# A two-layer decoder trunk: the even mixer's recurrent part is put in another order

## What is computed

```python
for i in range(DEPTH):                       # layer 0 is even, layer 1 odd; 512 tokens, width 1024
    x = x + 0.5 * swiglu(rms_norm(x, ffn1_norm[i]), ffn1_w_gu[i], ffn1_w_down[i])
    hn = rms_norm(x, mix_norm[i])
    if i % 2 == 0:
        proj = hn @ even_w_in[j]
        ya = sliding_window_attention(qa, ka, va, swa_sinks[j])          # 8 heads, 2 kv heads
        yb = rwkv7_time_mix(hb, ...)                                     # 8 heads of 64
        mixed = jnp.concatenate([ya, yb], axis=-1) @ even_w_out[j]
    else:
        mixed = forgetting_attention(qc, kc, vc, log_f) @ fox_w_out[j]
    x = x + mixed
    x = x + 0.5 * swiglu(rms_norm(x, ffn2_norm[i]), ffn2_w_gu[i], ffn2_w_down[i])
    x = x + jax.nn.sigmoid(rms_norm(x, ple_norm[i]) @ ple_w_gate[i]) * (p[i] @ ple_w_proj[i])
return rms_norm(x, final_norm)

def step(state, inp):                        # inside rwkv7_time_mix, over the tokens
    r_t, w_t, k_t, v_t, kk_t, a_t = inp
    s_kk = jnp.einsum('bhij,bhj->bhi', state, kk_t)
    state = (state * w_t[:, :, None, :] - s_kk[..., None] * (kk_t * a_t)[:, :, None, :]
             + v_t[..., None] * k_t[:, :, None, :])
    return state, jnp.einsum('bhij,bhj->bhi', state, r_t)
```

## Time and profile before

| | |
|---|---|
| median of three runs | 2234.67 us (2231.94 to 2236.96) |
| the profiled execution's own time | 2235.76 us |
| its span | 2234.1 us |
| TensorE busy | 2147.3 us, 96% of the span |
| VectorE, ScalarE, GpSimd busy | 1126.0, 746.0, 347.8 us |
| share of TensorE in the chain that ended last | 92% |
| mean granted TensorE clock | 0.981 |

### The profile page before, as it was taken

How to read it: one execution, slowest core, us unless ns; L and a number is a source line. 1 busy time by engine, 2 the same in 40 slices (tenths; PEclk the granted TensorE clock), 3 DMA queues, 4 the chain that set the end, 5 groups by cost and what they waited for, 6 DMA issues and landing times.

```text
span 2234.1 us, 32237 instructions
## 1 busy us (share of the span) xinstructions
PE 2147.3 (96%) x12522; PEld 1746.5 (78%) x12522; DVE 1126.0 (50%) x1337; ACT 746.0 (33%) x968; POOL 347.8 (16%) x352
## 2 busy tenths in 40 slices
PE   7999999996868999999999999999999899999998
PEld 6888888775857888888887888887667688888887
DVE  4443445556685644344565433445666454424464
ACT  4432223343122333122254422223444343312234
POOL 2000004444130300000330000013333320000032
PEclk9999999997979999999999999999999999999999
DMA  5323324320000433332333334324322143243232
GB/s 152 94 80 109 95 84 113 95 57 20 4 2 12 132 94 82 106 107 79 86 111 91 95 92 113 94 71 109 94 75 66 57 132 101 83 118 94 67 94 85
DMA packets 365116, 192.29 MB, mean 86 GB/s; under 512 B 9694, under 2 KB 362064, under 8 KB 365024
## 3 DMA queue, kind: packets, MB, share of 16 engines
q1 hardware_dynamic: 362784, 185.10, 30.0%
q0 software_dynamic: 2224, 5.86, 0.8%
q10 hardware_dynamic: 16, 0.00, 0.0%
HBM read 188.81 MB, written 2.13 MB: 85 GB/s over the span
## 4 chain that ended last, share of the span: by engine, by line
PE 92%; DVE 5%; ACT 2%; issue 1%; DMA 0%; POOL 0%; SPq 0%; ACTq 0%; POOLq 0%; DVEq 0%
PE bank L427 24%; PE bank L428 24%; PE bank L429 24%; PE bank L1182 3%; PE bank L1683 2%; PE bank L1685 2%; PE bank L1684 2%; PE bank L795 2%; PE bank L797 2%; PE bank L796 2%; PE bank L1700 1%; PE bank L1719 1%; PE bank L1730 1%; DVE w_lo L417 1%; ACT w_hi L412 1%
## 5 line engine op out<-in xcount | busy, mean ns | idle before, releaser
L427 PE MATMUL bank<-xn_hi,w_hi 128*128 128x512 f32 x1416 | 554.9, 392 | 10.9 <-DVE w_lo L2190 6.0
L428 PE MATMUL bank<-xn_hi,w_lo 128*128 128x512 f32 x1416 | 552.6, 390 | 0.0
L429 PE MATMUL bank<-xn_lo,w_hi 128*128 128x512 f32 x1416 | 552.4, 390 | 0.0
L412 ACT CAST w_hi<-w_raw 128x2048 fp32r<-128x2048 f32 (+3 forms) x211 | 336.3, 1594 | 624.0 <-PE bank L429 560.1
L417 DVE TENSOR_TENSOR w_lo<-w_raw,w_hi 128x2048 fp32r<-128x2048 f32 (+3 forms) x209 | 441.6, 2113 | 151.2 <-ACT w_hi L412 149.8
L427 PEld LDWEIGHTS bank<-xn_hi,w_hi 128*128 128x128 f32 x1416 | 266.9, 188 | 69.5 <-DVE w_lo L2190 6.3
L428 PEld LDWEIGHTS bank<-xn_hi,w_lo 128*128 128x128 f32 x1416 | 266.8, 188 | 56.1 <-issue 1.0
L429 PEld LDWEIGHTS bank<-xn_lo,w_hi 128*128 128x128 f32 x1416 | 266.8, 188 | 55.7
L429 PE MATMUL bank<-h_lo,w_hi 128*128 128x512 f32 x704 | 273.9, 389 | 0.0
L427 PE MATMUL bank<-h_hi,w_hi 128*128 128x512 f32 x704 | 273.9, 389 | 0.0
L428 PE MATMUL bank<-h_hi,w_lo 128*128 128x512 f32 x704 | 273.9, 389 | 0.0
(11 more groups left out here) (345 smaller groups left out, 2624.3 us busy)
## 6 DMA issues: line engine op xcount, KB each, us to landing
w_raw<-in_ffn_w_gu_dram SPq DMA_DIRECT2D x176, 512.0 KB, 5.0
w_raw<-in_ffn_w_down_dram SPq DMA_DIRECT2D x64, 384.0 KB, 3.9
w_raw<-in_ffn_w_down_dram SPq DMA_DIRECT2D x64, 320.0 KB, 3.7
w_raw<-in_even_w_in_dram SPq DMA_DIRECT2D x20, 512.0 KB, 4.5
w_raw<-in_ple_w_gate_dram SPq DMA_DIRECT2D x16, 512.0 KB, 3.8
w_raw<-in_fox_w_in_dram SPq DMA_DIRECT2D x16, 512.0 KB, 5.2
w_raw<-in_even_w_out_dram SPq DMA_DIRECT2D x16, 256.0 KB, 3.2
w_raw<-in_fox_w_in_dram SPq DMA_DIRECT2D x16, 256.0 KB, 4.3
```

The lines of the kernel that those rows point to most:

```text
L412: nc.scalar.copy(w_hi[slot][:, 0:tiles], w_raw[slot][:, 0:tiles]).then_inc(w_hi_ready, 1)
L427: nc.tensor.matmul(dst, w[0], hi[:, k], start=k == 0, stop=False)
L428: nc.tensor.matmul(dst, w[1], hi[:, k], start=False, stop=False)
L429: last = nc.tensor.matmul(dst, w[0], lo[:, k], start=False, stop=k == tiles - 1)
```

## The change

- **Projections in jobs of 8 tiles**: 20 jobs with one bank each, in place of 10 with two; the lora and hb tiles come in the order in which the front of half 0 needs them (`HB_TILES`). `FIRST_WINDOW, APART` become 27, 22.
- **Front of half 0** is put between the projection groups (`rwkv_front_*`, eight pieces on TensorE at groups 118 to 158, with two banks of its own that all eight pieces use in turn).
- **Front of half 1** is put between the inverse levels of half 0, its eight pieces on TensorE one or two to a level; `ab` and `ak` of half 1 stand inside and behind the chain of states of half 0.
- **Tail of half 0** is put between the inverse levels of half 1.
- **Inverse levels**: the level's mask is applied to A before the product, on GpSimd (`a_level`, ten operations of 128x512 in each half), and the product is only copied, by ScalarE (`x_copied`), where VectorE masked it before.
- **Buffers**: pairs of buffers for the two halves; `we` goes into the levels' buffer `m_x`; products that read two interleaved operands are issued as two of 64 columns.
- **Output projection, both mixers**: the weights of jobs 2 and 3 (and 6 and 7) are loaded and split into the upper half of their slot, so they needn't wait until jobs 0 and 1 are done. Job 0's six first rows are issued inside the last chain of states, job 1's ahead of the last `y_turned`.

The core of the diff:

```diff
+        bk = [placed(behind_projections, "bk0", HEADS_BY_DIM), placed(XN, "bk1", HEADS_BY_DIM)]
+        kr = [placed(behind_swa_v, "kr0", HEADS_BY_DIM), placed(XN + 8, "kr1", HEADS_BY_DIM)]
+        kf0 = [placed(behind_swa_k, "kf0_0", HEADS_BY_TOKEN), placed(Y + 28, "kf0_1", HEADS_BY_TOKEN)]
...
+        am0 = [placed(Y + 8, "am0_0", HEADS_BY_TOKEN), placed(behind_swa_v, "am0_1", HEADS_BY_TOKEN)]
+        am2 = [placed(Y + 24, "am2_0", HEADS_BY_TOKEN), placed(behind_swa_v + 4, "am2_1", HEADS_BY_TOKEN)]
+        bonus = [[placed(W + 44 + 2 * q, f"bonus0_{q}", [P, T]) for q in range(2)], [act_out, prod]]
...
+        m_x = placed(XN + 16, "m_x", [P, 2, 2, NC, C])
+        mt_inv = placed(XN + 24, "mt_inv", HEADS_BY_TOKEN)
+        a_lev = placed(XN + 28, "a_lev", HEADS_BY_TOKEN)
+        akm = placed(SCRATCH + 8, "akm", [P, 2, 2, NC, C])
...
+            for n, j, slot, _ in out_jobs(st):
+                e.wait_ge(w_ready, n - 1 if j < 2 else n - 3)
+                if st.startswith("even") and j in (2, 3):
+                    seen(e, ("gn_normed", "y_weighted")[j - 2], 1, 1)
+                loaded = (w_loaded_upper if upper(j) else w_loaded)[slot]
                 for k in (0, DT // 2):
-                    load_tiles(e, n, slot, k, DT // 2, rows[:, k:k + DT // 2, ds(j * P, P)])
+                    first = upper(j) * DT + k
+                    e.dma_start(w_raw[slot][:, first:first + DT // 2],
+                                rows[:, k:k + DT // 2, j * P:(j + 1) * P]).then_inc(loaded, 16)
...
-                return bank[(2, 6)[j]]
+                return bank[(1, 5)[j]]
...
-                product(out_bank_of(st, j, slot)[:], slot, 0, DT, y_hi, y_lo,
+                product(out_bank_of(st, j, slot)[:], slot, upper(j) * DT, DT, y_hi, y_lo,
...
+                if j + 2 < DT:
+                    out_split_hi(act, st, j + 2)
+                    gain_hi(act, norms[st] + 1, j)
...
+                if j + 2 < DT:
+                    out_split_lo(dve, st, j + 2)
...
-        FIRST_WINDOW, APART = 18, 24
+        R_TILE, K_TILE, V_TILE = 0, 1, 2
+        HB_TILES = [(t, 2 * h + q) for h in range(2) for t in (K_TILE, R_TILE, V_TILE) for q in range(2)]
+        LORA_JOB, HB_JOB, EVEN_JOBS = 2 + RP, 4 + RP, 4 + 4 * RP
+        FIRST_WINDOW, APART = 27, 22
...
+            firsts = [SWA_Q, SWA_Q + P] + [a * P for a in range(RP)] + [HB + 3 * RD, HB + 3 * RD + P]
+            firsts += [HB + hb_tile(i) * P for i in range(3 * RP)]
+            for j, col in enumerate(firsts):
+                n = base + j
                 e.wait_ge(w_ready, n - 1)
...
                 for g in range(first, last):
-                    n = base + g // (2 * DT)
-                    slot, k, t = n % 2, g % DT, g % (2 * DT)
-                    if t == 0:
+                    n = base + g // DT
+                    slot, k = n % 2, g % DT
+                    if k == 0:
...
+                    dst = bank[slot][:]
+                    hi, lo = w_hi[slot][:, k], w_lo[slot][:, k]
-                    if t == 2 * DT - 1:
+                    if k == DT - 1:
...
+            front = rwkv_front_tensor(pe, st, 0)
+            between = [(20, value_rows, ())]
             for a in range(RP):
-                begin = 4 * DT + FIRST_WINDOW + APART * a
...
+                begin = FIRST_WINDOW + APART * a
+                between += [(begin, logits, (a, 0)), (begin + 5, logits, (a, 1)),
+                            (begin + 32, transposes, (a, 0)), (begin + 36, transposes, (a, 1)),
+                            (begin + 40, times_values, (a,))]
+            between += [(g, part, ()) for g, part in zip((118, 122, 127, 131, 139, 145, 152, 158), front)]
...
-            for what in "J0 E0 J1 J2 C0 E1 H0 J3 C1 E2 J4 H1 J5 C2 E3 H2 J6 C3 J7 H3".split():
...
+            for what in ("J0 J1 T0 J2 J3 J4 E0 J5 J6 C0 J7 E1 T1 H0 J8 J9 C1 E2 J10 H1 J11 F0 J12 C2 E3 J13 H2 F1 F2 "
+                         "J14 F3 J15 F4 C3 F5 J16 H3 F6 J17 J18 F7 J19").split():
...
-            for what in "J0 L0 J1 D0 L1 J2 D1 V0 J3 M2 L2 J4 M3 D2 V1 L3 J5 M4 D3 V2 J6 M5 J7 M6 V3 M7".split():
...
+            for what in ("J0 J1 J2 L0 J3 J4 D0 J5 L1 J6 J7 T1 D1 V0 J8 L2 J9 M0 J10 M1 V1 D2 L3 J11 M2 J12 M3 V2 "
+                         "J13 M4 D3 M5 F0 J14 F1 F2 J15 F3 M6 F4 V3 J16 F5 M7 F6 F7 F8 J17 M8 F9 J18 M9 F10 "
+                         "J19 M10 M11").split():
...
-            for what in "N0 S2 N1 S3 S4 N2 S5 N3 S6 S7".split():
...
+            for what in "N0 N1 S0 S1 S2 N2 S3 S4 S5 N3 S6 F0 S7 F1 S8 F2 F3 S9 S10 S11".split():
...
+            def ss():
+                for q in range(2):
+                    seen(pe, "kk_squared", h, q)
+                    seen(pe, "v_by_token", h, q)
...
+            def x_copied(h, level):
+                for q in range(2):
+                    level_seen(act, "x", h, level, q)
+                    if level > 1:
+                        level_seen(act, "mxt", h, level - 1, q)
+                    nc.scalar.copy(m_x[:, q, 1], by_chunk(rb(q, 2)[:])).then_inc(R["x_copied"], 1)
...
+            def a_level(h, level):
+                for q in range(2):
+                    if level > 1:
+                        level_seen(pool, "x", h, level - 1, q)
+                    elif h:
+                        level_seen(pool, "x", 0, LEVELS - 1, q)
+                    nc.gpsimd.tensor_tensor(a_lev[:, q], am0[h][:, q], over_chunks(masks[:, MASK_LT + level]),
+                                            ALU.mult).then_inc(R["a_level"], 1)
...
+                ak(0, q)
+            aab(0)
+            f(0)
+            front[0]()
+            xs(0, 1)
+            front[1]()
+            ms(0, 1)
+            front[2]()
+            xs(0, 2)
+            ms(0, 2)
+            front[3]()
+            xs(0, 3)
+            ms(0, 3)
+            front[4]()
+            xs(0, 4)
+            ms(0, 4)
+            front[5]()
+            xs(0, 5)
+            front[6]()
+            ms(0, 5)
+            front[7]()
+            w_and_e(0)
+            gq(0)
+            hs(0)
+            yc(0)
+            z(0, 1)
+            z(0, 2)
+            ab(1, 0)
+            z(0, 3)
+            z(0, 4)
+            ab(1, 1)
+            z(0, 5)
+            z(0, 6)
...
+            f(1)
+            xs(1, 1)
+            yz(0, 0)
+            ms(1, 1)
+            xs(1, 2)
+            yz(0, 1)
+            ms(1, 2)
+            xs(1, 3)
+            g(0)
+            ms(1, 3)
+            xs(1, 4)
+            ms(1, 4)
+            y_turned(0)
+            xs(1, 5)
+            ms(1, 5)
...
+            yc(1)
+            for c in range(1, NC - 1):
+                z(1, c)
+                if c > 1:
+                    out_begin(pe, st, 0, c - 2, c - 1)
+            out_begin(pe, st, 0, NC - 3, OUT_BEGUN["even"])
+            yz(1, 0)
+            yz(1, 1)
+            g(1)
+            out_begin(pe, st, 1, 0, OUT_BEGUN["even"])
+            y_turned(1)
...
+            front = rwkv_front_vector(dve, st, 1)
+            ab_masked(0)
+            ak_masked(0)
+            start_inverse(0)
+            front[0]()
+            level_done(0, 1)
+            front[3]()
+            front[1]()
+            level_done(0, 2)
+            front[4]()
+            front[2]()
+            front[5]()
+            level_done(0, 3)
+            front[6]()
+            front[7]()
+            front[8]()
+            level_done(0, 4)
+            front[9]()
+            front[10]()
+            level_done(0, 5)
+            gq_copied(0)
+            states(0)
+            ab_masked(1)
+            ak_masked(1)
+            start_inverse(1)
...
+            front = rwkv_front_pool(pool, st, 1)
+            start_inverse(0)
+            a_level(0, 1)
+            diag(0)
+            a_level(0, 2)
+            front[0]()
+            a_level(0, 3)
+            a_level(0, 4)
+            front[1]()
+            a_level(0, 5)
+            front[2]()
+            front[3]()
+            start_inverse(1)
+            a_level(1, 1)
+            diag(1)
+            for level in range(2, LEVELS):
```

1257 lines of the change are left out of this document (725 added, 532 removed).

## The result

| | before | after |
|---|---|---|
| median, us | 2234.22 (2231.94 to 2236.96, 4 runs) | 2209.51 (2203.80 to 2211.84, 4 runs) |
| the profiled execution's own time | 2235.76 | 2211.56 |
| its span | 2234.1 | 2209.9 |
| mean granted TensorE clock | 0.981 | 0.989 |

The ratio is 0.9885, 95% interval 0.9861 to 0.9909. The forecast was 2203 us, in a range of 2183 to 2223. Two executions of the later runs, one of the kernel before and one of e11_together, took 2729 and 2752 us at a mean granted clock of 0.745 and 0.731; they are left out of the ratios.

The account below looks back on a forecast made before the run. Prediction: TensorE bounds projections and cores, VectorE and chains between engines bound fronts and tail. Terms -9.4 + 2.5 + 12.1 + 2.6 - 42.5 + 9.3 - 3.1 - 3.3 = -31.8 gave 2203 us, range 2183 to 2223.

Parts of the forecast that it names:

- What stood between the cores: From half 0's chain of states to half 1's first x: 52.5 us falls to about 10, -42.5.
- the third: Rival: the first front doesn't overlap, its shared banks making pieces wait; part 1 takes 184.0, kernel 2224 us; chance 0.08.
- part 1: Projections with the first front: 172.1 us falls to 162.7, -9.4.
- Rivals 2 and 4: VectorE and GpSimd block one another, 2215 us, chance 0.15; GpSimd becomes the bound, 2239 us, chance 0.07.
- The new waits: Waits the new order adds in projections and first front: 19.1 us in all, slow clock included.
- The base: Projections and first front without the new waits: 133.7 us plus 9.9 for the front's matmuls at full clock.
- TensorE stays the bound: Rival: most new waits vanish, part 1 gains 22.5 and levels cost less; kernel 2179 us; chance 0.15.
- the first wait: In the projections, before job 2: TensorE waits 3.2 us for VectorE, 5.0 with 1.8 of slow clock.
- The levels: Half 0's inverse levels with the second front: 39.3 us in place of 27.2, +12.1, from following VectorE's and GpSimd's work.
- the floor: Least cost of the second front in half 0's levels: TensorE's own work, +8.2 us.
- Second levels: Half 1's levels to the end of `yz`: +9.3 us, of it 7.8 for the tail and 1.5 for six groups.
- The out projection: Even mixer from the end of `yz` to out job 2: -3.1 us; fox mixer's wait removed: -3.3.

Follow-up runs that it names:

- e11_together: Changed kernel with queue orders mended in projections and levels, four banks for the first 14 projection jobs, value_rows and logits pieces moved: 2189.09 us, ratio 0.9797.
- the mended kernels: Changed kernel with the order at the end of the projections mended on four engines (2196.84 us), and later runs built on it, down to 2187.29 us.
- e6_part1_order: Changed kernel with the order at the end of the projections mended on TensorE, ScalarE, VectorE and GpSimd: 2196.84 us, ratio 0.9828.
- the last run: e11_together with GpSimd's a_level(0,3) ahead of a_decayed and VectorE's last two mixing steps behind ab_masked(0): 2187.29 us, ratio 0.9793.
- e12_groups_behind_chain: Changed kernel with the six groups of out job 0 behind the last chain of states, not in its steps: 2209.88 us, ratio 0.9891.
- e2_front0_behind: Changed kernel with the front of half 0 behind the projections again on all five queues: 2211.46 us, ratio 0.9897.
- e3_front1_between: Changed kernel with the front of half 1 between the cores again, behind half 0's chain of states: 2220.44 us, ratio 0.9937.
- e9: Changed kernel with four steps of the second front made on VectorE for one chunk of eight, result not the reference's: 2207.92 us, ratio 0.9882.
- e4: Changed kernel with GpSimd's a_lev products made for one chunk of eight from level 2 on, result not the reference's: 2205.72 us, ratio 0.9871.
- e8: Changed kernel with the earlier out-projection job code back in both mixers, early-begun groups left in place: 2215.90 us, ratio 0.9917.

## Why the prediction came out as it did

**The bulk was right, for its reason.** What stood between the cores fell by 44.3 us for 42.5. The run with the second front between the cores again gives 10.9 us back, by this place alone; the new place of half 0's tail had no run of its own. Of the rivals the third came nearest: as the change wrote it, the first front's overlap brought 3.1 us of part 1, and the kernels' times can't tell it from nothing. But without it part 1 takes 173.7, not the 184.0 I had worked out, and the order made it, not the shared banks, which the mended kernels share too. Rivals 2 and 4 asked for GpSimd operations of 1.9 and 3.0 us; in half 0's levels 17 took 26.0, 1.5 each. Under them lay a misreading of the earlier trace rows: the two masks of 4.67 us have 1024 elements, so they take 1.17 for each 512, no longer than the 1.25 of the pair at 560.60. Beside these masks only VectorE lost.

**Part 1 is the term that was mis-sized**: -9.4 forecast, -1.4 measured. Its parts by their own measure. The new waits sum to 15.3 us; the forecast's, without the clock, were 14.0. That is nearly right, by luck: the 3.3 us before `logits(2,1)` were 1.7 and the 3.3 before `ss` none, and in their place came the 3.49 and 3.77, two queue orders I had not followed to the end (C3 behind F4 on ScalarE; M8 behind GpSimd's masks). The base is told by e11_together: its 149.2 less 2.2 us of waits is 147.0 without any, where 133.7 + 9.9 gave 143.6. What is left of 170.6 after 147.0 and 15.3 is 8.4 for the lower clock, where I had 5.1. `ss` alone is 1.6 of it. Its 16 products of 2 columns stand at 3.41 us in the timeline above; in e6_part1_order they are:

```profile
511.36 1.84 PE L1234 MATMUL bank<-head_ones,bk 128*128 128x2 f32 x16
```

The granted clock is 0.50 in the first case and 1.00 in the second. Of the base's 3.4 little is the front: in e11_together its eight pieces take 10.3 us from their starts to the next group's, for the 9.9 I had. The other 3.0 are the projections and the attention, 136.7 us for 133.7; their stream of groups is interrupted 30 times where it was 21, and what this costs was not tried. 1.3 + 3.3 + 3.4 is 8.0, the miss of 7.9. And the rival "TensorE stays the bound", for which this part would be 149.6, was nearer than its chance of 0.15 says: the order and two more banks brought 149.2. The agreement is partly chance, since the 149.6 still holds the first wait.

**The levels: right size, for the most part by the wrong reason.** The steps said VectorE; the runs say TensorE for all but 2.15 us. The front costs it 11.0 us there, where I had named 8.2 as the floor. Those 8.2 were the front's busy time times the mean granted clock of the whole stretch, idle time included, less the first piece; that came near between the projection groups and not here, and why the same pieces cost more between the levels the runs don't show. The 2.15 us are the wait of level 3 and the clock behind it. The forecast had the place of that wait (`a_decayed` ahead of level 3's `a_level`); the last run shows VectorE's front work holding the same x, so this part was right for its reason.

**Second levels: 4.8 us too small.** The levels themselves came as told (+7.9 for 7.8), in sum: the waits in them were not compared one by one. The six groups cost 3.8 for 1.5, as e12_groups_behind_chain shows: I had taken a step's wait for free time of TensorE. And from `we` to the chain it took 2.5 us longer, 1.5 in half 0, where I had written 0. Timeline of TensorE there, both halves:

```profile
612.46 0.30 PE L1482 MATMUL bank<-vtok,ktok 64*64 64x64 f32 x4 [1.45 <-issue]
...
674.83 0.27 PE L1482 MATMUL bank<-m_x,btok 64*64 64x64 f32 x2 [1.49 <-issue]
```

These stalls end in nothing that a semaphore shows. With 0.33 and 0.82 further on they make 1.8 and 2.3 us, for 0.8 and 0.3 before; that is 1.0 of the 1.5 us and 2.0 of the 2.5. The columns are the same, as I had counted; the instructions are not: 511 matmuls for 390, since products of 128 columns are two of 64 now. That the stall comes from the supply of instructions fits this and was not tried.

**The out projection: too small by 2.3 us** in sum (7.2 for 6.4, and some 1.5 behind fox job 2), for the most part by the clock behind the waits.

## What to carry to other kernels

When work is woven into a full stage, first follow each engine's queue for who waits behind an instruction that waits, three engines deep: here a dozen instructions set elsewhere in their queues, and two more banks, were worth 20 us, nearly as much as the change. Mend all links of such a chain before judging the idea, since one link alone only moves the wait. When a stage seems bound by one engine, add up the busy time and the waits of the other: here TensorE's 37.23 and 0.86 us made the 38.09 exactly, while VectorE, busy 38.0 of 40.2 us in the changed kernel, had looked like the bound. And an instruction may wait for two engines at once; moving the later one only uncovers the other.

## What the runs showed of the chip

The mean granted clock of a stretch with idle time in it is not the clock of every product in it. The first front of the kernel before has 0.65 over its 34.4 us, and 1.00 from 530.3 to 532.3 us, where its 16 products of 2 columns ran in 1.84 us. At 0.50, 16 such products took 3.41 us in the changed kernel and 3.54 in e2_front0_behind and e3_front1_between. So these products, too, take nearly twice as long at the lower clock.

The same instructions gave two times, 3 us apart, for group 118 to `ab`: 60.2, 60.3 and 60.4 in the changed kernel, e9 and e12, and 57.3, 57.5 and 57.3 in e3, e4 and e8. All have the wait of 3.49 us. Windows behind it in e4_no_a_level, then in the changed kernel:

```profile
508.00:512.00 4.00, 4.00 (x20) 3.51 (x19) 2.98 (x5) 1.16 (x4) 2.05 (x2) 0.64 0.44 131
512.00:521.00 9.00, 9.00 (x64) 7.28 (x64) 1.40 (x6) 1.53 (x2) 0.00 (x0) 1.00 0.01 2
```
```profile
508.00:512.00 4.00, 3.58 (x16) 3.05 (x16) 3.86 (x6) 1.43 (x5) 2.93 (x2) 0.67 0.44 129
512.00:521.00 9.00, 9.00 (x51) 7.69 (x52) 0.57 (x4) 0.00 (x0) 0.00 (x0) 0.58 0.01 3
```

In one the clock is at the lower of its two levels (1.2 and 2.4 GHz) for some 3 us, in the other for some 10. So one wait's price in clock varies from execution to execution, and a forecast that gives it as one figure has this much spread in each. In the mended order the granted clock of this stretch was 1.00, and five kernels gave 45.13 to 45.15 us: without waits the spread goes too.
